# The first norm of a two-layer diffusion step: where its scale vectors, condition rows and sums of squares are computed

## The reference, cut to what matters

```
m    = silu(cond) @ mod_w[0] + mod_b[0]          # 9 vectors of 1024, for context and for latent
xn   = rms_norm(h, norm_g[0,0]) * (1 + scale) + shift     # scale = m[1], shift = m[0]
h    = h + 0.5 * gate * ((silu(xn @ w_gate) * (xn @ w_up)) @ w_down)   # gate = m[2]; hidden width 2816
```

## Time and profile before

| | us |
|---|---|
| median of 3 runs (lowest, highest) | 1565.73 (1563.63, 1567.07) |
| profiled execution, its own time | 1569.92 |
| its span | 1568.1 |
| TensorE matmul busy | 1526.7 (97%) |
| VectorE busy | 1074.0 (68%) |
| ScalarE busy | 616.8 (39%) |
| GpSimd busy | 73.9 (5%) |

### The profile page before, as it was taken

One profiled execution on the slowest core, in us unless ns is written; L12 is line 12 of the kernel. 1 busy time (PEld: TensorE's weight loads), 2 busy tenths in 40 slices (PEclk: granted clock), 3 DMA queues, 4 the chain that ended last, 5 costly groups with the idle time before them and its releaser, 6 DMA issues.

```text
span 1568.1 us, 23354 instructions
## 1 busy us (share of the span) xinstructions
PE 1526.7 (97%) x9159; PEld 1497.4 (95%) x9159; DVE 1074.0 (68%) x1423; ACT 616.8 (39%) x840; POOL 73.9 (5%) x59
## 2 busy tenths in 40 slices
PE   6899999989989999999999999999999999999999
PEld 6899999979848999999999999999999999999999
DVE  6786677868896876677887767787777557443323
ACT  3352332254474552332246332225643246333221
POOL 2000000013100200000020000002000010000000
PEclk9999999989999999999999999999999999999999
DMA  9235556645223245455623555663552532333332
GB/s 386 88 136 199 202 202 214 234 177 202 94 71 135 81 149 221 166 213 216 241 102 141 198 203 188 238 243 113 205 220 83 215 108 94 133 122 134 132 112 91
DMA packets 49937, 262.68 MB, mean 168 GB/s; under 512 B 6608, under 2 KB 7888, under 8 KB 27984
## 3 DMA queue, kind: packets, MB, share of 16 engines
q1 hardware_dynamic: 49872, 261.79, 45.3%
HBM read 259.54 MB, written 2.23 MB: 167 GB/s over the span
## 4 chain that ended last, share of the span: by engine, by line
PE 78%; DVE 7%; issue 5%; ACT 4%; DMA 4%; SPq 1%; POOL 1%; DVEq 0%; ACTq 0%; POOLq 0%
PE ps L1286 23%; PE ps L1287 23%; PE ps L1288 23%; DMA raw<-panels 2%; DVE mprod L827 2%; PE ps L1320 2%; PE ps L1321 2%; PE ps L1323 2%; ACT w_hi L537 2%; DVE w_lo L819 1%; DMA raw_x<-panels 1%; PE ps L1513 1%; DVE x_lo L890 1%; DVE h L1011 1%; PE ps L1606 1%
## 5 line engine op out<-in xcount | busy, mean ns | idle before, releaser
L819 DVE TENSOR_TENSOR w_lo<-raw,w_hi 128x2048 fp32r<-128x2048 f32 x163 | 373.3, 2290 | 308.8 <-ACT w_hi L537 307.2
L537 ACT ACTIVATE w_hi<-raw 128x2048 fp32r<-128x2048 f32 x164 | 314.4, 1917 | 654.8 <-PE ps L1288 475.4
L1286 PE MATMUL ps<-x_hi,w_hi 128*128 128x384 f32 (+1 forms) x1520 | 516.3, 340 | 10.5 <-DVE x_lo L890 8.8
L1287 PE MATMUL ps<-x_lo,w_hi 128*128 128x384 f32 (+1 forms) x1520 | 513.4, 338 | 0.0
L1288 PE MATMUL ps<-x_hi,w_lo 128*128 128x384 f32 (+1 forms) x1520 | 513.0, 337 | 0.0
L827 DVE SCALAR_TENSOR_TENSOR mprod<-mraw,cB 128x1024 f32<-128x1024 f32 x256 | 313.3, 1224 | 7.8
L1286 PEld LDWEIGHTS ps<-x_hi,w_hi 128*128 128x128 f32 x1520 | 287.0, 189 | 14.4 <-issue 7.4
L1287 PEld LDWEIGHTS ps<-x_lo,w_hi 128*128 128x128 f32 x1520 | 287.0, 189 | 0.7
L1288 PEld LDWEIGHTS ps<-x_hi,w_lo 128*128 128x128 f32 x1520 | 286.7, 189 | 0.0
L1288 PE MATMUL ps<-act_hi,w_lo 128*128 (+1 forms) x832 | 279.6, 336 | 0.0
L1286 PE MATMUL ps<-act_hi,w_hi 128*128 (+1 forms) x832 | 279.6, 336 | 0.0
(11 more groups left out here) (154 smaller groups left out, 1161.9 us busy)
## 6 DMA issues: line engine op xcount, KB each, us to landing
raw<-panels SPq DMA_DIRECT2D x164, 1024.0 KB, 5.1
mraw<-mod_rows SPq DMA_DIRECT2D x128, 512.0 KB, 3.5
raw_x<-panels SPq DMA_DIRECT2D x5, 1024.0 KB, 5.8
mshift<-mod_rows SPq DMA_DIRECT2D x8, 512.0 KB, 15.6
mscale<-mod_scale SPq DMA_DIRECT2D x6, 512.0 KB, 12.3
bias<-na_bias SPq DMA_DIRECT2D x4, 512.0 KB, 5.8
h<-x_in_t SPq DMA_DIRECT2D x1, 1536.0 KB, 11.1
out<-h SPq DMA_DIRECT2D x4, 384.0 KB, 2.3
```

The costliest lines, as they stand in the source:

```text
L537: nc.scalar.activation(w_hi[q0 % 2][:, :], raw[q0 % 2][:, :], ACT.Copy).then_inc(hi_done, 1)
L819: nc.vector.tensor_tensor(w_lo[q0 % 2][:, :], raw[q0 % 2][:, :], w_hi[q0 % 2][:, :].bitcast(F32), ALU.subtract).then_inc(lo_done, 1)
L1286: mm(out, w[0][:, cols], xs[0], start=start, stop=False)
L1287: mm(out, w[0][:, cols], xs[1], start=False, stop=False)
```

## The change

All 8 scale tiles go to TensorE. The condition rows are loaded once into one partition of `raw[1]` (8 KB) and spread to all partitions by four matmuls with a row of ones, into PSUM banks 0 to 3; ScalarE's SiLU reads them there and writes `cB`. The loads are reordered: the scale tiles and the first shift tiles first, shift tiles 4 to 7 last, and panel 1 behind a wait for the spreading (it lands in the same buffer). VectorE sums 8 shift tiles, and adds the squares itself instead of GpSimd, behind the last x tile; it also writes the two shift columns of x_hi. Pair 0's products are ordered anew: gate of tile k beside up of tile k - 2. The sum over the partitions and the spreading of the norm move from pair 0 into pair 1, and so does pair 0's eviction, which needs them.

```diff
-PE_TILES = 6
-SUM_TILES = 2 * KD - PE_TILES
+SUM_TILES = KD
+SCALE_TILES = ((0, 5), (5, 8))
...
-            sp.dma_start(mscale[:, 0, :], mod_scale[0]).then_inc(mscale_in[0], 16)
-            sp.dma_start(cB[:, :, :], cond_rows.rearrange("(o c) k -> o c k", o=1).to_broadcast([P, 2, D])).then_inc(cb_in, 16)
...
+            sp.dma_start(raw[1][0:1, :], cond_rows.rearrange("(o c) k -> o (c k)", o=1)).then_inc(cb_in, 16)
+            shift_tile(0)
+            scale_tile(0)
             sp.dma_start(vec[:, :], vecs).then_inc(vec_in, 16)
-            mod_first(1)
+            scale_tile(1)
+            shift_tile(1)
+            scale_tile(2)
+            scale_tile(3)
+            shift_tile(2)
+            scale_tile(4)
+            shift_tile(3)
             sp.dma_start(h[:, :, :], x_in_t).then_inc(x_in, 16)
+            scale_tile(5)
+            panel(0, 0)
+            scale_tile(6)
+            spare_panel(0)
+            scale_tile(7)
             sp.dma_start(ident[:, :], eye).then_inc(const_in, 16)
+            for k in range(4, KD):
+                shift_tile(k)
+
+            sp.wait_ge(cb_pe, 1)
             gate_up(0)
...
 GpSimd: norm()
-                for k in range(1, last):
+                for k in range(1, last if n else 0):
...
 ScalarE
-            act.wait_ge(cb_in, 16)
-            nc.scalar.activation(cB[:, :, :], cB[:, :, :], ACT.Silu).then_inc(cb_done, 1)
-            squares(0)
+            act.wait_ge(cb_pe, 1)
+            nc.scalar.activation(cB[:, :, :].rearrange("p c k -> p (c k)"), ps[:, 0:4, :].rearrange("p b k -> p (b k)"), ACT.Silu) \
+                .then_inc(cb_done, 1)
+            act.wait_ge(x_in, 16)
+            act.wait_ge(mvec, 5)
+            for k in range(5):
+                scaled(k)
             split(0, 0)
+            for k in range(2):
+                square_first(k)
             split_spare(0)
-            for k in range(KD):
-                act.wait_ge(mvec, k + 1)
-                nc.scalar.activation(x_hi[:, k, T:XT], modT[:, k, :], ACT.Copy)
+            act.wait_ge(mvec, KD)
+            for k in range(5, KD):
                 scaled(k)
+            for k in range(2, KD):
+                square_first(k)
+            split(1, 0)
+            split(2, 0)
             ffn(0)
...
 VectorE
+            dve.wait_ge(mod_pe, 1)
+            for k in range(3):
                 shift_sums(k)
+            first_scale(0)
+            shift_sums(3)
+            first_shift(slice(0, 4))
             for k in range(4):
+                low_first(k).then_inc(x_done, 1)
+            split(0, 0)
+            low_first(4)
+            split_spare(0)
+            first_scale(1)
+            for k in range(4, KD):
+                if k > 4:
+                    low_first(k)
                 shift_sums(k)
+                first_shift(slice(k, k + 1)).then_inc(x_done, 1)
+            split(1, 0)
+            for k in range(1, KD):
+                dve.wait_ge(sq_done, k + 1)
+                if k > 1:
+                    dve.wait_ge(acc_done, k - 1)
+                nc.vector.tensor_tensor(sqsum[:, 0:T], sq[:, 0, :] if k == 1 else sqsum[:, 0:T],
+                                        sq[:, k, :] if k < 4 else tmp[:, k - 4, 0:T], ALU.add).then_inc(acc_done, 1)
+            split(2, 0)
+            dve.wait_ge(acc_done, KD - 1)
+            dve.wait_ge(const_in, 16)
             ffn(0)
...
 TensorE
+            def first_products():
+                pe.wait_ge(lo_done, 1)
+                gate(0)
+                gate(1)
+                pe.wait_ge(spare_lo, 1)
+                for k in range(2, KD):
+                    up(k - 2)
+                    last = gate(k)
+                last.then_inc(pe_done, 1)
+                up(KD - 2)
+                up(KD - 1).then_inc(spare_pe, 1)
+
+            def second_products():
+                g, u = gate_panel(0, 1), up_panel(0, 1)
+                pe.wait_ge(lo_done, g + 1)
+                feature_major(g, gate_bank(1), [(0, k) for k in range(KD)], XT)
+                norm_sums_beside(0)
+                feature_major(g, gate_bank(1), [(1, k) for k in range(KD)], XT).then_inc(pe_done, 1)
+                norm_spread(0)
+                pe.wait_ge(lo_done, u + 1)
+                pe.wait_ge(ms_done, 1)
+                feature_major(u, up_bank(1), [(1, k) for k in range(KD)], XT)
+                pe.wait_ge(gs_done, 1)
+                feature_major(u, up_bank(1), [(0, k) for k in range(KD)], XT).then_inc(pe_done, 1)
+
+            pe.wait_ge(ones_set, 3)
+            pe.wait_ge(cb_in, 16)
+            for j in range(4):
+                last = mm(ps[:, j, :], ones[0:1, :], raw[1][0:1, 512 * j:512 * j + 512], start=True, stop=True)
+            last.then_inc(cb_pe, 1)
+            for k in range(KD):
                 mod_scale_tile(k)
-            pe.wait_ge(const_in, 16)
-            pe.wait_ge(ones_set, 3)
+            pe.wait_ge(cb_done, 1)
             ffn(0, 0)
```

More of the change, by code:

```diff
@@ L925, in pair @@
                     if g0 == 0:
[L926 removed]
+                        if f:
+                            split(gate_panel(f, 1), 0)
                         factor(NORM_OF[f])
@@ L1056, in from_pe @@
-            def from_pe(half):
-                ks = slice(PE_TILES // 2 * half, PE_TILES // 2 * half + PE_TILES // 2)
-                dve.wait_ge(mod_pe, PE_TILES // 2 * (half + 1))
-                first_scale(ks, ps[:, 6 + half, 0:PE_TILES].rearrange("p (k c) -> p k c", c=2))
+                link(nc.vector.tensor_tensor(modT[:, ks, :], shsum[:, ks, :], mbT[:, ks, None].to_broadcast([P, n, 2]), ALU.add))
+                link(nc.vector.tensor_copy(x_hi[:, ks, T:XT], modT[:, ks, :]))
+                return nc.vector.tensor_tensor(x_lo[:, ks, T:XT], modT[:, ks, :], x_hi[:, ks, T:XT].bitcast(F32), ALU.subtract)
@@ new lines, in first_scale @@
+            def first_scale(half):
+                lo, hi = SCALE_TILES[half]
+                dve.wait_ge(mod_pe, hi)
+                scale = ps[:, 6 + half, 0:2 * (hi - lo)].rearrange("p (k c) -> p k c", c=2)
+                link(nc.vector.tensor_tensor(aT[:, lo:hi, :], scale, mb1[:, lo:hi, None].to_broadcast([P, hi - lo, 2]), ALU.add))
+                nc.vector.tensor_tensor(aT[:, lo:hi, :], aT[:, lo:hi, :], ngT[:, lo:hi, None].to_broadcast([P, hi - lo, 2]),
+                                        ALU.mult).then_inc(mvec, hi - lo)
@@ L1061, in low_first @@
             def low_first(k):
                 dve.wait_ge(xh_done, k + 1)
[L1063 to L1067 removed]
+                for cond, cols in ((0, CTX), (1, LAT)):
+                    last = nc.vector.scalar_tensor_tensor(x_lo[:, k, cols], h[:, k, cols], aT[:, k, cond:cond + 1],
+                                                          x_hi[:, k, cols].bitcast(F32), ALU.mult, ALU.subtract)
@@ L1078, in _ @@
-            split(0, 0)
-            shift_sums(4)
-            split_spare(0)
-            low_first(0)
-            shift_sums(5)
-            low_first(1)
-            first_shift(slice(4, 6))
-            from_pe(1)
-            low_first(2)
-            late(6)
-            late_vectors(6)
-            low_first(3)
-            low_first(4)
-            late(7)
-            late_vectors(7)
-            for k in range(5, KD):
-                low_first(k)
+                low_first(k).then_inc(x_done, 1)
@@ L1297, in mod_scale_tile @@
                 pe.wait_ge(mscale_in[k], 16)
-                half, at = divmod(k, PE_TILES // 2)
+                half = 0 if k < SCALE_TILES[0][1] else 1
+                at = k - SCALE_TILES[half][0]
                 for kk in range(KD):
@@ L1467, in ready_ffn, with tile, gate, up @@
                 return waits
-            for k in range(PE_TILES):
+            def first_products():
+                def tile(bank, w, k, a):
+                    return three(ps[:, bank + a, 0:XT], w, slice(256 * k + P * a, 256 * k + P * a + P),
+                                 (x_hi[:, k, :], x_lo[:, k, :]), k == 0, k == KD - 1)
+                def gate(k):
+                    pe.wait_ge(x_done, k + 1)
+                    return [tile(gate_bank(0), slot(0), k, a) for a in range(2)][-1]
+                def up(k):
+                    return [tile(up_bank(0), (hi_x, lo_x), k, a) for a in range(2)][-1]
+                pe.wait_ge(lo_done, 1)
[26 more added lines that the diff above has]
+            for k in range(KD):
                 mod_scale_tile(k)
-            pe.wait_ge(const_in, 16)
-            pe.wait_ge(ones_set, 3)
+            pe.wait_ge(cb_done, 1)
             ffn(0, 0)
```

57 lines of the change are left out of this document (21 added, 36 removed).

## The result

The changed kernel takes 1577.61 us (median of 4 runs, 1577.25 to 1581.7), the kernel before 1566.23 (median of 4, 1563.63 to 1567.07): a ratio of 1.0087, with a 95% interval of 1.0073 to 1.0101. It is 11 us slower, where 1.4 us faster was forecast, and the upper end of the range (1568.8) is 9 us too low.

The account below looks back on a forecast made before the run. Loads and VectorE bound the start, TensorE the rest. Earlier splits gave -3.0 us against the profiled 1569.92 (1566.9); over all clock-rise positions, 1 to 2 us under the 1565.73 median: 1564.3, range 1560.5 to 1568.8.

Parts of the forecast that it names:

- the disputed term: Start, spreading and scale tiles: TensorE's clock rises at 8.4 us, falls some 3.4 us later; tile 5 done at 24.9.
- rival 1: Start: clock stays at half through spreading and scale tiles; tile 5 at 27.8, time 1568.8 us; chance 0.25.
- the rivals' last sentence: Spreading: weight-load time hangs on columns, not rows, so one row would cost and count like 128; no run shows it.
- a rise as forecast: Clock going from half to full in the second half of the condition's spreading, at 8.4 us.
- VectorE's chain: Start: VectorE's sums, low parts and splits after tile 5, putting the last x tile at 50.8 us against 54.6.
- the split of panel 2 done ahead: VectorE in pair 0: this split with its wait, 2.6 us, is done early, so later panels' splits come sooner.
- The waits: Pairs 1 to 3: TensorE waits for VectorE's splits, about 2.7 us at panel 3, 1.9 at 4, 1.0 at 6.
- a fall only in pair 0: Clock dropping while pair 0 waits for x; none was expected, and one would have shown the forecast wrong.
- Rival 2: Pairs 1 to 3: a 2 to 3 us delay in ScalarE's part or the norm leaves 1565.7 us; chance 0.13.
- the lead of pair 0: TensorE ahead by up to five us, pair 1 done at 72.4 instead of 81.1, then lost waiting for splits.
- Rival 3: Start: scale tiles, 28 us without a gap, keep or lift the clock; tile 5 at 21, 1561 us; chance 0.12.

Follow-up runs that it names:

- Experiments 1 and 2: Changed kernel plus 32, 64 or 96 unused bytes: 1569.27, 1576.97, 1568.13 us; kernel before with `scsum` allocated last: 1574.71 us.
- a_k128: Changed kernel with its 32 bytes back and the condition's spreading matmuls using all 128 rows (127 of zeros): 1568.66 us, one run.
- a_pad32: Changed kernel with 32 unused bytes per partition ahead of `cB`, putting the tiles back in place: 1569.27 us, ratio 1.0027.
- experiment 4: Not the network: 48 stretches of 48 products, activations 32 bytes higher each stretch, weights 32 bytes higher in the last 16; steps 173.3 to 176.6 ns.
- a_norm0: Changed kernel with 32 bytes back, condition broadcast, squares on ScalarE summed early by GpSimd, partition sums in pair 0: 1564.39 us, ratio 0.9995.

## Why the prediction was wrong, step by step

**The term that was missing.** The sum had no line for the place of the tiles. It followed each instruction that is added, removed or moved, and said that from pair 4 on TensorE "is the bound and keeps it". The order there did stay the same; the price of a product did not. Some 6000 products of 384 columns at about 2 ns make 12.3 us, those of 256 columns add 0.7, and those of 386 columns take 1.2 less: 11.8 in all, of which 8.9 fall behind 556 us, where nothing else differs. Experiments 1 and 2 measured 8 to 9 in the median for the whole kernel, so some 3 us do not come out there. In the two profiled executions the changed kernel regained 2.6 us around the attention stage (414 to 455 us, clock 0.88 before and 1.00 after). Whether it does so in the median is not settled, for these falls come and go: the kernel with the weights moved has the same slow steps, and its clock read 0.88 there too.

**Which clock?** This was named as the disputed term, and went to the forecast with 0.50; rival 1 had 0.25 and is what happened. The spreading took 7.16 us (6.8 forecast), cB was ready at 12.2 (11 to 12), and no record of it or of the scale tiles ran faster. Tile 5 came to VectorE at 27.5 (rival 1: 27.8, forecast: 24.9), the last x tile was done at 53.1 (53.7, 50.8), the first eviction began at 67.46 (67.6, 64.6). The error was to let the f32 work of attention, matmuls of 64 and 128 rows, speak for matmuls of one row. That one row of weights would cost and count like 128, as the rivals' last sentence has it, is right for the cost (0.85 us a pass in both) and wrong for the clock. a_k128, one run, shows that a rise as forecast, at full clock from 11.8 us, does come with 128 rows. Since its passes also began 3 us later, that the rows alone made the difference rests on this one execution. Even so it did not pay, for the load had to wait for the zeros and TensorE began at 6.14.

**The price of a late start.** Against an execution of the kernel before with the clock's fall, rival 1 came to no difference; against one without it, to 3.1 us. The profiled executions of its variants bear this out: panel 6's split is at 104.1 and 104.3 in the two with a fall after 54 us, and at 100.4 to 101.0 in the five without one. The changed start gave 104.8 to 105.1 every time. Rival 1's 3.1 us is close to the measured 4.2 of a_pad32 (interval 1.7 to 6.7). Its 1568.8 is within 0.5 us of that kernel's 1569.27: had the 32 bytes not moved, this rival would have been right, and the time still 0.5 us above my range.

**VectorE's chain.** Up to x it was right except for its starting point: scale vectors to last x tile was forecast at 25.9 us and took 25.6. The additions took 4.4 us (4.0 forecast) and the splits 2.3 each. Behind the first eviction one term was mis-sized: the split of panel 2 done ahead was to save 2.6 us up to panel 6. It saved 1.7 (from the first eviction to panel 6's split 37.6 us, 39.3 before), since VectorE now waits 0.92 us for ScalarE at act_lo (72.39 above), where the split had stood. With this, rival 1's panel 6 would have been at 105.1 instead of 104.2; it was at 105.04.

**The waits.** Forecast 2.7, 1.9 and 1.0 us at panels 3, 4 and 6; measured 3.15, 2.07 and none. At panel 6 there was none: the clock fell at 90.5 us, after a stretch with 4.43 us of work in 6.5, and the twelve products of the next 3.4 us took 1.3 us more than at full clock, which is more than the wait that was forecast. I had looked for a fall only in pair 0, where there was none, as forecast.

**Rival 2** named a delay in ScalarE's part, and the 0.92 us are one, if smaller than its 2 to 3 us; and the lead of pair 0 was lost in pairs 1 to 3. **Rival 3** (full clock in the tiles) did not happen in any run with this start.

**The chances.** 0.18 for slower all came from the start. Nothing in the trace of before shows what a shift by 32 bytes does; but "this edit also changes the memory map" could be read from the diff, and it would have widened the range upwards.

## What to carry to other kernels

Compare addresses as well as instructions: when a change adds, drops or resizes a tile ahead of those that a matmul streams, first put the same number of bytes back and measure that kernel, and judge the edit itself by it. When the span grows steadily through code that the edit does not touch, count the records in equal, fully busy stretches, and take starts, not durations. An analogy for the clock is worth only as much as the shapes have in common: rows, columns and gaps.

## What the runs showed of the hardware

- The step of TensorE's products of 384 f32 columns depends on the distance between the streamed tile and the weights in a partition, modulo 256 bytes: from 173.3 ns at 32 to 176.6 at 96 (experiment 4), 1.9%. By the Trainium skill ("SBUF — State Buffer", section "SBUF: two separate sides") only the port pair shared by VectorE and GpSimd causes contention among the engines, and TensorE has its own ports. The trace does not contradict it: TensorE alone was at work in experiment 4, so the 3.3 ns between the best and the worst distance are not between engines.
- Eight f32 passes with one row of weights, without a gap for 7.16 us, left the clock at half in all four profiled executions; with 128 rows it was at full after 5.66 us of them (a_k128, one execution). 128 scale records of two columns never raised it in 27.47 us, and in a_k128 it fell while they ran. By the Trainium skill ("TensorE: Matmul & The Clock Gate", section "What's actually happening") the clock is throttled by default and activity releases it. The trace of the changed kernel disagrees for these two shapes: TensorE was busy from 3.15 to 37.7 us, and all of it ran at half.
- While GpSimd added tiles in SBUF, VectorE's instructions with two inputs there took longer: one sum 1.90 us instead of 1.22, eight low parts 4.21 instead of 2.72 (a_norm0). By the Trainium skill ("SBUF — State Buffer", section "Who interferes with whom") a VectorE instruction with two SBUF inputs contends with a GpSimd instruction that reads SBUF, and the trace agrees.
